# Running sums of stick-breaking attention: key blocks from the last to the first, with the sum of the later blocks added on VectorE

## The reference

```python
z = jnp.einsum('bhqd,bhkd->bhqk', q_i, k) * scale
mask = kpos[None, :] < qpos[:, None]
log_fail = jnp.where(mask, jax.nn.log_sigmoid(-z), 0.0)
later = lax.cumsum(log_fail, axis=3, reverse=True) - log_fail
a = jnp.where(mask, jnp.exp(jax.nn.log_sigmoid(z) + later), 0.0)
return jnp.einsum('bhqk,bhkd->bhqd', a, v)
```

## Time and profile before

| | us |
|---|---|
| Median of three runs | 2915.82 |
| The profiled execution | 2914.18 |
| Its span | 2912.0 |
| TensorE busy in the span | 2796.6 |
| VectorE busy | 1410.5 |
| ScalarE busy | 964.0 |
| GpSimd busy | 533.2 |

### The profile page before, as it was taken

The page is one execution under the profiler, slowest core; times in us unless marked ns, Lnnn a source line. Parts: engine busy times, 40 slices in busy tenths (PEclk is TensorE's granted clock), DMA queues, the critical chain, the costliest instruction groups (busy, mean ns, idle before and its releaser), DMA issues.

```text
span 2912.0 us, 33354 instructions
## 1 busy us (share of the span) xinstructions
PE 2796.6 (96%) x13978; PEld 2244.8 (77%) x13978; DVE 1410.5 (48%) x2076; ACT 964.0 (33%) x1278; POOL 533.2 (18%) x414
## 2 busy tenths in 40 slices
PE   7998989999999999999999999899999998999998
PEld 4776657888887888888888877688888875788886
DVE  6645546666544333373222455555345365454453
ACT  3435444322233322243222333432223244332222
POOL 2563301100112201221001100012012100021121
PEclk9999989999999999999999999999999999999999
DMA  6322103456332222222632322122322311222321
GB/s 240 123 88 92 54 8 145 174 183 222 139 100 92 91 85 79 76 87 100 172 116 70 119 81 81 40 101 86 108 101 74 115 58 66 73 93 76 114 83 69
DMA packets 51093, 296.36 MB, mean 102 GB/s; under 512 B 6617, under 2 KB 6745, under 8 KB 25088
## 3 DMA queue, kind: packets, MB, share of 16 engines
q1 hardware_dynamic: 44912, 276.58, 27.1%
q0 software_dynamic: 4736, 15.34, 2.0%
q10 hardware_dynamic: 1296, 2.32, 0.2%
HBM read 283.46 MB, written 8.65 MB: 100 GB/s over the span
## 4 chain that ended last, share of the span: by engine, by line
PE 88%; DVE 5%; ACT 4%; issue 1%; POOL 1%; DMA 0%; SPq 0%; DVEq 0%
PE ps L218 88%; DVE wlo L211 1%; PE ps L1312 1%; ACT whi L200 1%; DMA F<-in_ada 0%; ACT F L1329 0%; DVE F L412 0%; DVE hl L416 0%; DVE ada L460 0%; DVE F L2260 0%; ACT L253 0%; ACT E L2833 0%; DVE F L827 0%; ACT E L2831 0%; ACT hh L430 0%
## 5 line engine op out<-in xcount | busy, mean ns | idle before, releaser
L218 PE MATMUL ps<-hh,whi 128*128 128x512 f32 x2088 | 829.6, 397 | 12.4 <-ACT F L2811 5.8
L218 PE MATMUL ps<-hl,whi 128*128 128x512 f32 x2088 | 815.4, 391 | 0.0
L218 PE MATMUL ps<-hh,wlo 128*128 128x512 f32 x2088 | 814.6, 390 | 0.0
L211 DVE TENSOR_TENSOR wlo<-raw,whi 128x2048 fp32r<-128x2048 f32 (+2 forms) x235 | 497.3, 2116 | 509.3 <-ACT whi L200 509.2
L218 PE MATMUL ps<-R,whi 128*128 128x512 f32 x2080 | 650.0, 391 | 8.0 <-DVE wlo L211 3.1
L200 ACT ACTIVATE whi<-raw 128x2048 fp32r<-128x2048 f32 (+2 forms) x235 | 409.6, 1743 | 686.2 <-PE ps L218 681.7
L218 PEld LDWEIGHTS ps<-hh,whi 128*128 128x128 f32 x2088 | 393.1, 188 | 103.7 <-issue 12.2
L218 PEld LDWEIGHTS ps<-R,whi 128*128 128x128 f32 x2080 | 390.5, 188 | 95.3 <-issue 6.9
L218 PEld LDWEIGHTS ps<-hl,whi 128*128 128x128 f32 x2088 | 393.0, 188 | 83.2
L218 PEld LDWEIGHTS ps<-hh,wlo 128*128 128x128 f32 x2088 | 393.4, 188 | 82.2 <-issue 3.3
L218 PE MATMUL ps<-R,wlo 128*128 128x512 f32 x1040 | 404.7, 389 | 0.0
(11 more groups left out here) (343 smaller groups left out, 2587.5 us busy)
## 6 DMA issues: line engine op xcount, KB each, us to landing
F<-in_ada SPq DMA_DIRECT2D x32, 1024.0 KB, 4.9
raw<-in_fs0in SPq DMA_DIRECT2D x22, 1024.0 KB, 6.1
raw<-in_fs1in SPq DMA_DIRECT2D x22, 1024.0 KB, 4.8
raw<-in_fc0in SPq DMA_DIRECT2D x22, 1024.0 KB, 4.9
raw<-in_fc1in SPq DMA_DIRECT2D x22, 1024.0 KB, 4.8
Rf<-in_ada0h SPq DMA_DIRECT2D x24, 512.0 KB, 3.5
raw<-in_fs0out SPq DMA_DIRECT2D x16, 704.0 KB, 4.5
raw<-in_fs1out SPq DMA_DIRECT2D x16, 704.0 KB, 4.1
```

The source lines that it names most:

```text
L211: e.tensor_tensor(m.wlo[n % 2][:, 0:size], m.raw[m.slot[n]][:, 0:size], m.whi[n % 2][:, 0:size].bitcast(F32), SUB).then_inc(*s.up("wlo", n))
L218: return e.matmul(out, l, r, start=start, stop=stop, skip_group_check=True)
```

## The change

Step 4 to step 7 now go through the blocks in the order c = 3, 2, 1, 0. Block c gets one product of `tril` with its own sp, and one product of ones with sp of block c + 1, in which VectorE has in the meantime added sp of the blocks behind it, in place (`sb_later`, for c = 2 over 128 columns and for c = 1 over 256). That is 7 matmuls of 128, 256 + 128, 384 + 256 and 512 + 384 columns. The in-place addition waits for the `tril` product of the same block (`sb_own`), which reads the block's own sp. The subtraction moves into a helper. The scheduler's table gets new durations for the four steps.

```diff
         yield step("pe:0.5 dve:0.7", ("six", "sb_z", h, 3), done=("scores", h))
-        for work in ("act:3.9", "dve:1.7", "pe:2.2"):
+        for work in ("act:3.9", "dve:1.7"):
             yield step(work)
-        yield step("pe:1.3", ("six", "sb_sub", h, 1), "dve:1.3")
-        yield step("pe:0.7")
-        yield step("pe:0.3 dve:0.7", ("six", "sb_sub", h, 3))
+        yield step("pe:0.3", ("six", "sb_sub", h, 3), "dve:0.3")
+        yield step("pe:0.7", beside="dve:1")
+        yield step("pe:1.1", ("six", "sb_sub", h, 1), "dve:0.4")
+        yield step("pe:1.5 dve:0.7", beside="dve:0.5")
         yield step("act:1.3")
...
             s.wait_ge("sb_sp", h)
-            for c in range(4):
+            for c in (3, 2, 1, 0):
                 if c % 2:
                     six_free(s, "sb_sub", h, c)
                 elif c:
-                    s.wait_ge("sb_sub", h, 0)
+                    s.wait_ge("sb_z", h, 2)
                 else:
-                    s.wait_ge("sb_z", h, 2)
-                for j in range(c, 4):
-                    w = T - j * P
-                    t = mm(e, m.ps[5 + c % 2][:, T - c * P - w:T - c * P], m.k("tril" if j == c else "ones"), stick_sp(m, j), j == c, j == 3)
+                    s.wait_ge("sb_sub", h, 2)
+                t = mm(e, m.ps[5 + c % 2][:, 0:T - c * P], m.k("tril"), stick_sp(m, c), True, c == 3)
+                if c < 3:
+                    t.then_inc(*s.up("sb_own", h, c))
+                    if c < 2:
+                        s.wait_ge("sb_later", h, c + 1)
+                    t = mm(e, m.ps[5 + c % 2][:, P:T - c * P], m.k("ones"), stick_sp(m, c + 1), False, True)
                 t.then_inc(*s.up("sb_cum", h, c))
                 yield
...
-            s.wait_ge("sb_sub", h, 3)
+            s.wait_ge("sb_sub", h, 0)
             e.activation(stick_z(m), stick_z(m), table(e, s, ACT.Exp)).then_inc(*s.up("sb_w", h))
...
-            for c in range(4):
-                s.wait_ge("sb_cum", h, c)
-                a = stick_z(m, c)
-                e.tensor_tensor(a, a, m.ps[5 + c % 2][:, 0:T - c * P], SUB).then_inc(*s.up("sb_sub", h, c))
+            for c in (2, 1):
+                s.wait_ge("sb_own", h, c)
                 if c == 1:
-                    yield from steps(2)
+                    s.wait_ge("sb_later", h, 2)
+                a = stick_sp(m, c)[:, P:]
+                e.tensor_tensor(a, a, stick_sp(m, c + 1), ADD).then_inc(*s.up("sb_later", h, c))
+                for i in (c + 1, c) if c == 2 else ():
+                    dve_stick_sub(e, s, m, h, i)
+                yield
+            for c in (1, 0):
+                dve_stick_sub(e, s, m, h, c)
```

More of the change, by code:

```diff
@@ L41 @@
     "dve_delta": "corner conv l2 gate_rows ab token_gate beta kb qd dec vb kdec lt at mask0 triT tri state go",
-    "pe_stick": "sb_sum sb_score sb_cum sb_pv",
+    "pe_stick": "sb_sum sb_score sb_own sb_cum sb_pv",
     "act_stick": "sb_sq sb_t sb_rs_ln sb_rs sb_exp sb_w sb_hi",
-    "dve_stick": "sb_q sb_z sb_sp sb_sub sb_lo",
+    "dve_stick": "sb_q sb_z sb_sp sb_later sb_sub sb_lo",
     "act_latent": "lq_sq lk_sq lq_rs_ln lq_rs lq_hi lk_rs_ln lk_rs lk_hi qn rope_x mv",
@@ L2782, in pe_stick_heads @@
                 s.wait_ge(V_BY[t % 2], "stick", 1, t)
-            s.wait_ge("sb_sub", h, 2)
+            s.wait_ge("sb_sub", h, 0)
             s.wait_ge("sb_w", h)
@@ L2829, in act_stick_heads @@
             if h:
-                s.wait_ge("sb_cum", h - 1, 3)
+                s.wait_ge("sb_cum", h - 1, 0)
             e.activation(stick_sp(m), stick_z(m), ACT.Abs).then_inc(*s.up("sb_exp", h, 0))
@@ L2868, in dve_stick, with dve_stick_sub @@
         yield from steps(2)
+def dve_stick_sub(e, s, m, h, c):
+    s.wait_ge("sb_cum", h, c)
+    a = stick_z(m, c)
+    e.tensor_tensor(a, a, m.ps[5 + c % 2][:, 0:T - c * P], SUB).then_inc(*s.up("sb_sub", h, c))
 def dve_stick_heads(e, s, m):
```

## The result

The changed kernel takes 2920.26 us (median of 12 runs, 2918.2 to 2925.1); the kernel before, run beside it, 2917.6 (12 runs, 2911.79 to 2924.92). The ratio is 1.0018, with a 95% interval of 1.001 to 1.0027: slower by a little under 0.2%, where 0.14% faster (a range of 2908 to 2915 us) was forecast. Against this the kernel before also ran 1.8 us higher than the median of three that the forecast started from. The profiled execution took 2919.0 us, its span 2917.0, 4.8 and 5.0 more than before.

A forecast was written before the change was run, and what follows sets the result against it. TensorE (96% busy) was taken as the bound, at the end two serial chains. Columns -7.8 and stalls +3.0 gave -4.8 us, the chain -3.1; -4.2 taken from 2914.18, plus 1.6, gave 2911.6 us (2908 to 2915).

The forecast's parts named there:

- Columns, -7.8 us: TensorE, running sums of 8 heads: 512 fewer matmul columns a head at 1.76 ns; 0 to 8.4 us won, 7.8 taken.
- its last sentence: If TensorE's busy time fell much less than 7 us, the column price was wrong or the lower clock ate it.
- Additions, nothing as work, 0 to 0.4 us a head as turns: VectorE, two in-place additions per head: free as work, 0.4 us a head if covers fail, 0.8 at the slower price.
- Rival (c): No change, 2915.0 us: additions held up by GpSimd in heads 0 to 3 give 3.4 us back; chance 0.15.
- Three stalls, 3.0 us: TensorE waits: head 1 for L2811 0.9 us more, head 2 for bank 6 0.5, head 3 before the values 1.6.
- The chain's start of head 6, 399.5 us: Head 6 starts 3.3 us late, from 396.17: wins 0.6 and 1.8, delta head 3's levels cost 2.5, pair 3's norm 3.2.
- Rival (b): About 7 us slower, 2922.7 us: head 6 starts late behind pair 3's norm and delta head 3's slow levels; chance 0.15.
- Head 6, 24.9 us long: Head 6 shrinks from 30.2 us by 5.3, as delta head 3's levels leave it and its own columns fall.
- Head 7, from its sums to the exponential 7.4: Head 7's sums stand alone at the lower clock: 7.4 us to the exponential instead of 8.6, 1.2 less.
- The sum: Whole kernel: -4.8 us by TensorE's account, -3.1 by the chain of heads; -4.2 taken.
- What moves: Section on the new order's effects: three TensorE stalls in heads 1, 2 and 3, together 3.0 us.

The follow-up runs named there:

- e5: Changed kernel without its additions: same order of steps and blocks, ones run again over every later block (10 products a head); 2921.02 us, ratio 1.002.
- e2: Sums of the kernel before (10 matmuls, blocks 0 to 3), every engine in the changed kernel's order; 2923.85 us, ratio 1.0026.
- e9: e3 with head 6 begun at once and delta head 3's steps 26 to 56 spread beside heads 6 and 7; 2911.47 us, ratio 0.9992.
- e11: e9's order with the sums of the kernel before, no additions; 2922.23 us, ratio 1.0024.
- e7: e6 with unread constant products in three more TensorE waits: behind delta head 1 and around the end of delta head 3's inverse; 2911.83 us, ratio 0.9987.
- e1: Changed kernel's new sums, additions and subtractions in the old order of steps, one modulation step moved; 2923.42 us, ratio 1.0027.
- e3: Changed kernel with the last six steps of pair 3's projection (norm and DMA swap) moved beside steps 5 to 9 of head 5; 2917.19 us, ratio 0.9998.
- e4: Changed kernel with unread constant products in TensorE's waits of head 7, five before its sums, two before its values; 2917.55 us, ratio 1.0003.
- e6: Changed kernel with e3's early norm and e4's constant products together; 2916.06 us, ratio 0.9999.
- e8: Kernel before with two constant products in one wait of head 7, instruction for instruction the same up to head 7; 2916.3 us, ratio 0.9997.
- e10: e9 with six constant products in the wait behind delta head 1; 2909.57 us, ratio 0.998.

## Why the prediction was wrong

- **Columns, -7.8 us:** right in size. In one order the new products save 3.9 us of busy TensorE (changed against e5), 6.7 (changed against e2) or 8.7 (e9 against e11), with 3.0, 5.3 and 8.3 of stage. The page shows 2.4. e2 against before has 4.8 more busy time for the same matmuls at a lower clock, which fits the gap; the prediction named that reading in its last sentence, but put no price on it.
- **Additions, nothing as work, 0 to 0.4 us a head as turns:** right in the sum. They are dearer than taken (0.37 and 0.57 us in the mean, 0.285 and 0.417 assumed), because of two of the sixteen: 1.56 us at 203.90, beside a GpSimd operation on SBUF tiles that began at 203.29, and 0.93 us at 319.72, beside one that began at 318.89. The others took 0.27 to 0.43. The Trainium skill (SBUF — State Buffer, "Who interferes with whom") says that a VectorE instruction with two SBUF inputs contends with a GpSimd instruction that reads SBUF; these two rows agree. TensorE waited for an addition once (0.97 us, a weight load in head 0), and without them (e5) nothing is won. Rival (c) falls.
- **Three stalls, 3.0 us:** the first was well sized as a wait (5.3 to 6.6; 6.2 forecast), but its second price was missed, the low clock of the 5 us behind it (225.3 to 230.6; e7 has it at full clock). The second, at head 2, was 0.16 us where 0.5 was forecast, and the third, at head 3, 1.1 where 1.6 was. But the waits for exponentials grew from 1.5 to 5.4 us over the stage, 2.2 of it at head 7; the forecast had them at head 3 alone.
- **The chain's start of head 6, 399.5 us: this step failed.** It came at 404.38. Its parts can be compared one by one. Head 5's last step on VectorE ended at 393.50, where the sum implies 391.2: 2.3 us late (by what is taken up below). From there to the end of the norm's last multiplication it took 5.7 us, where 3.9 was implied: 1.8 more. The sum had laid the norm's operations (3.2 us) on engines that were otherwise free; in truth the exponential for k stood on ScalarE, and then the multiplication on VectorE, behind the end of delta head 2. From the multiplication to head 6 it took 5.2 instead of 4.3, with the last DMA at 3.23 instead of 2.36: 0.9 more. Together these are the 4.9 us that it came late.
- **Rival (b)** had this place, a deciding point of 404.5 (its sign, a start beyond 404, was met) and a time of 2922.7; the measured time came within 2.5 us of it. Heads 6 and 7 won back 3.0 us (51.8 to 48.7), where it had 2.5. But its mechanism was another: it had the levels of delta head 3 at the lower clock, 3.0 us each, while in the trace they ran at full clock (1.12 + 0.68 us), and head 6 waited for the norm. So its good number is in part luck.
- **Head 6, 24.9 us long:** 26.7. **Head 7, from its sums to the exponential 7.4:** 7.7 (440.01 to 447.74). Not foreseen were the 4.03 us of its values, at the low clock (0.57 from 449 to 453 us) after a 2.17 us wait.
- **The sum.** "What moves" charged the new order with 3.0 us on TensorE's account. With the old sums, e2 against before measures 0.26% of the time, 7.6 us, and 11.9 in the stage: the term was mis-sized by a factor of 2.5 to four. The stage's growth of 6.7 us (255.6 to 262.3) is 11.9 for the order and then 5.3 less for the products; taken the other way round (e1) it is 10.0 for the products and then 3.3 less for the order. That work and order depend on each other stood in no term of the prediction.

Why did the change lose time? Shown: the late norm, since the time is that of before once it is early (e3, 5.8 us by the ratios). Shown in head 7 itself, and repeated in e4, e6 and e7: the low clock there costs some 4 us (14.6 us from its softplus to the projection instead of 18.6 and 18.4). That the two add up is not shown (e6). The rest is seen in that e3 only equals before, though its sums should be cheaper, and it can be placed only in part. From one head's softplus to the next, the changed kernel takes longer than before in two places: from head 3 to head 4, 44.1 us against 38.8 (41.1 in e8), with TensorE busy 41.3 against 35.5 us (37.7), and from head 5 to head 6, 39.1 against 33.2 (34.4). It takes less from head 6 to head 7, 23.6 against 28.0 (24.9). So part of this is only work that moved forward; how much of it is loss stays open. That head 7 stood bare is not shown to be a cause (e9).

## What to carry to other kernels

Where a cost table drives the order of all engines, a change to one step is two changes: run the work in the old order and the old work in the new order, and price each, before believing either. Don't expect the prices to add up: here the new work lost 10 us of stage in the old order and gained 5 in the new one and 8 in a third. After a reorder, read the granted clock behind each longer wait of TensorE: where it fell, the wait is paid a second time by the matmuls behind it at half clock, and a few products into a free bank in the wait can be worth trying. The best versions, e10 (2909.57 us, ratio 0.998, 0.9968 to 0.9992) and e7 (2911.83, 0.9987), keep the new sums, have the norm early and fill the wait behind delta head 1.

## What the runs showed of the hardware that was not expected

- Twelve entries of constant products (5.32 us) in a 6.55 us wait took the granted clock of the 8 us after it from 0.56 to 1.00. With five constant products before the sums of head 7 and two before its values, the values took 2.34 us instead of 4.03.
- A bare wait of 2.2 us before the same values went with the low clock in the changed kernel (4.03 us) and with the full clock in e9 (2.34 us).
- The same instructions saw the clock fall at different places in two executions (0.97 and 0.65 from 380 to 390 us in e3 and e6), and the stretch from head 5 to head 6 differed by 4 us. Between before and e8, also the same instructions up to there, head 6's start differed by 5.8 us. That alone is as large as most effects studied here.
